# Last norms and gate of a decoder layer moved between the experts: rows in order of the later of their two experts

## The chip, the cores and the metric

The kernel runs on one core of one Trainium2 chip. The time is device time in microseconds (us) of one execution. The engines are TensorE (PE, matrix products; PEld is its loading of the stationary operand), VectorE (DVE), ScalarE (ACT), GpSimd (POOL) and SyncE (SP). Each runs its own list of instructions in order and waits for the others by semaphores. Sixteen DMA engines move data between HBM and SBUF, on behalf of SP's queue, ACT's queue and POOL's queue.

## The reference, cut to what matters

520 tokens (512 of a prompt, 8 of decoding) of width 1024 go through one layer and a last norm:

```python
m, new_buf, new_state = mixer(rmsnorm(h, g_mix), ...)        # convolution and retention heads
h = h + m
# hier_moe: top 1 of 4 groups, then top 2 of the 8 experts in it
u = rmsnorm(h, g_ffn)
for e in range(N_EXPERTS):                                    # 32
    hid = jax.nn.silu(u @ w_gate[e]) * (u @ w_up[e])          # 1024 -> 512
    y = y + cw[:, e:e + 1] * (hid @ w_down[e])                # 512 -> 1024
h = h + y
gate = jax.nn.sigmoid(rmsnorm(h, g_ple) @ w_ple_gate)         # 1024 x 1024
h = h + (p @ w_ple_proj) * gate                               # p: 256 wide, per token
y_prompt, y_sample = rmsnorm(h, g_final)
```

cw is zero for all but two experts of a token. All is float32. The weights of the 32 experts are 201 MB.

## The kernel before, in words

The **head** (to about 265 us) computes the mixer and the router, with the rows' transposes as moving operand and weights split into a high and a low part (fp32r, three products for one). At its end h lies in `xh` (token rows) and, as half rows of 512 values, in `h_rows` in HBM. The router gives for each expert the list of up to 64 rows that chose it (`index`, a row of a tile of 64; the two halves of a row lie on two partitions, so a tile is 128 x 512).

The **expert stage** takes the experts in order 0 to 31. Per expert, PE runs `gate_up` (16 matmuls of 512 columns for each of two units of weights), `hidden_t` (2 transposes), `rows_t` (4 transposes of the next expert's rows), `down` (8 matmuls, a third unit). ACT applies silu and copies the result out (`evac_out`, L908), DVE multiplies and copies (`mult_up`, `evac_h`, `evac_rows`). POOL gathers the rows of expert e+2 out of `h_rows` (L721) and scatters the result of expert e to `y_rows` in HBM (L727), which has a place for each token and each of its two choices. SP's queue loads the weights, 2 MB a unit, three units an expert. A unit is asked for as soon as the unit before it in its place has been used (`wait_ge(used[...])`). Ten places hold units at first, six ("ring", L573) from about unit 20 on. The pieces of `p @ w_ple_proj` are computed in experts 6 to 14 (L1668).

The **tail** starts when the last scatter has landed: `combine` adds the two results of each token (y_rows loaded in token order), the rows are transposed (L1938), the gate product runs in three fp32r products of 512 columns (L1964), with w_ple_gate split into high and low by ACT and DVE (L927, L1548), then sigmoid, the added projection, the last norm, and the store, for one tile of 8 and four tiles of 128 tokens. w_ple_gate is asked for at L610 behind the last expert's weights.

Order is written out by hand on each engine; there is no planner. An overflow branch (`n_over > 0`) handles experts with more than 64 rows.

Of the kernel before, what the change touches and what calls it, by code (L numbers as in the profile page):

```python
# [15 lines left out]
F32 = mybir.dt.float32  # L16
# [76 lines left out]
TAIL_TILES = [NT - 1] + list(range(NT - 1))  # L93
TAIL = [("u", 0), ("u", 1), ("pg", 0)]
for _n in range(1, NT):
    TAIL += [("pa", _n)] + ([("u", _n + 1)] if _n + 1 < NT else []) + [("pb", _n)]
TAIL.append(("pc", NT - 1))
GATES = [_job for _job in TAIL if _job[0] != "u"]
PARTS = [(_t, _q) for _t in range(NT - 1) for _q in range(2)] + [(NT - 1, 0)]
PART_FROM = 3  # L100
PART_PAIRS = -(-len(PARTS) // 2)
SPIN_TAIL, SPIN_ROWS = 52, 8


def columns_of(kind, n):

    last = n == NT - 1
    return dict(pa=slice(0, 512), pb=slice(512, 768 if last else D), pc=slice(768, D), pg=slice(0, D))[kind]


def gates(n):

    return sum(_job[1] < n for _job in GATES)

# [21 lines left out]

HEAD, REST = Plan(JOBS), Plan(TAIL)

# [5 lines left out]
GATE_SLOTS = PAIR_SLOTS[0:2]  # L144
# [8 lines left out]
def build(nc, a, o):  # L153
# [10 lines left out]
    y_tok = y_rows.rearrange("(t k) c -> t (k c)", k=2)  # L164

    with ExitStack() as ctx:
# [12 lines left out]
        def halves(ap):  # L179
# [26 lines left out]
        small = sb("small", [P, 240])  # L206
        stats = sb("stats", [P, 48])
# [10 lines left out]
                    valx=5, x0=1, y0=1, eps=1, io64=ROWS, io32=NE, rs=2, vm=4)  # L218
# [4 lines left out]
        assert at <= 240  # L223
# [43 lines left out]
        def mix_hi(k):  # L267
# [3 lines left out]
        gate_hi = [at_r(f"gate_hi{i}", UNIT, ring_at + slot * UNIT * 4)[:, :]  # L271
                   for i, slot in enumerate(PAIR_SLOTS[3:5])]
        gate_lo = [at_r("gate_lo0", UNIT, ring_at + PAIR_SLOTS[2] * UNIT * 4)[:, :], None]
        gate_lo_1 = [at_r("gate_lo10", UNIT // 2, region_d_at)[:, :],
                     at_r("gate_lo11", UNIT // 2, region_m_at + UNIT // 2 * 4)[:, :]]
        u3_hi = [at_r(f"u3_hi{i}", D, ring_at + (PAIR_SLOTS[5] * UNIT + i * D) * 4)[:, :] for i in range(2)]
        u3_lo = [at_r(f"u3_lo{i}", D, ring_at + (PAIR_SLOTS[5] * UNIT + (2 + i) * D) * 4)[:, :] for i in range(2)]
        mixT = region_m[:, :].rearrange("p (k t) -> p k t", k=KD)
        qk = region_q[:, 0:8 * T].rearrange("p (h t) -> p h t", h=8)
        pp = region_q[:, 0:NT * D].rearrange("p (t c) -> p t c", t=NT)  # L280
# [11 lines left out]
        g_fin_b = region_q[:, NT * D:NT * D + D]  # L292
        rs = [col["rs"][:, i:i + 1] for i in range(2)]
        lt16 = meanw[:, :].bitcast(F16).rearrange("p (s c) -> p s c", s=2)
        pT = trig[:, :].rearrange("p (k t) -> p k t", k=2)
# [69 lines left out]
        y_buf = [region_v[:, 0:2048], region_m[:, 0:2048]]  # L365
        u3T = [region_u[:, i * D:(i + 1) * D] for i in range(2)]
        gate = [region_u[:, 2 * D + i * D:3 * D + i * D] for i in range(2)]

        def gate_low(half, k):

            part, at = (gate_lo[0], k * 512) if half == 0 else (gate_lo_1[k // 4], k % 4 * 512)
            return part[:, at:at + 512]

# [26 lines left out]
        late_loaded, p_loaded = sem("late_loaded"), sem("p_loaded")  # L402
# [10 lines left out]
        over_hot_done, over_placed, over_done = sem("over_hot_done"), sem("over_placed"), sem("over_done")  # L413
# [12 lines left out]
        xh_loaded = [sem(f"xh_loaded{t}") for t in range(NT - 1)]  # L426
        y_loaded = [sem(f"y_loaded{i}") for i in range(2)]
        hy_done, hy_root, hy_rstd = sem("hy_done"), sem("hy_root"), sem("hy_rstd")
        gate_hi_ready, gate_lo_ready = sem("gate_hi_ready"), sem("gate_lo_ready")
        u3_ready, u3_hi_ready = sem("u3_ready"), sem("u3_hi_ready")  # L430
        pp_done, pp_made = sem("pp_done"), sem("pp_made")
        pe_tail, act_tail, dve_tail = sem("pe_tail"), sem("act_tail"), sem("dve_tail")
        part_square, part_sum = sem("part_square"), sem("part_sum")
        f_done, f_root, y_done, y_stored = sem("f_done"), sem("f_root"), sem("y_done"), sem("y_stored")
# [5 lines left out]
        def pair_fill(i, j):  # L440

            def fills(n, slot):

                return sum(16 * (PIECES if u in PIECED else 1) for u in range(n + 1) if EARLY_HOMES[u] == slot)

            if isinstance(i, int) and i < EARLY_PAIRS:
                home = EARLY_HOMES[i * 6 + j]
                if home in range(RING):
                    return home, fills(i * 6 + j, home)
                return home, 16 * len(spare[int(home[1])]) * EARLY_HOMES[:i * 6 + j + 1].count(home)  # L450
            slot = PAIR_SLOTS[j]

            return slot, i * 16 + (fills(len(EARLY_HOMES) - 1, slot) - (EARLY_PAIRS - 1) * 16)
# [3 lines left out]
        def parts_of(i, b):  # L457

            if not isinstance(i, int) or not PART_FROM <= i < PART_FROM + PART_PAIRS:
                return []  # L460
            at = (i - PART_FROM) * 2 + b
            return [at] if at < len(PARTS) else []

        def part_psum(n):

            return ps[:, 5 - n % 2, :]

        block = ctx.enter_context(nc.Block())


        @block.sync
        def _(sp):
# [126 lines left out]
            for j in range(6):  # L599
                unit, slot = NE * 3 - 6 + j, PAIR_SLOTS[j]  # L600
                sp.wait_ge(used[j % 3], NE - 2 + (j // 3 - 1))
                if j < 4:
                    load_unit(unit, slot)
# [1475 lines left out]
```

## Time and profile before

| | |
|---|---|
| time, median of 3 runs | 817.34 us (817.06 to 819.39) |
| profiled execution, span | 815.4 us |
| PE busy, DVE, ACT, POOL | 722.4, 288.1, 180.5, 102.8 us |
| DMA, all queues | 260.36 MB |
| mean granted TensorE clock | 0.986 |

The span is from the first to the last instruction; the median of the timed runs is 1.9 us above it. The profile shows three stages: the head with PE nearly always busy, the expert stage with the DMA engines nearly always busy, and the tail from 739 us on, with little DMA.

### The profile page before, as it was taken

Reading aid. Unit: us, or ns where it says so; the run is one execution under the profiler, and the core shown is the slowest. Engines: PE = TensorE matmul, PEld = TensorE weight load, DVE = VectorE, ACT = ScalarE, POOL = GpSimd, SP = SyncE. Lnnn points to the kernel's source line nnn. Section 1 sums busy time; section 2 is a strip of 40 time slices with the busy share of each in tenths; the row PEclk is TensorE's granted clock in tenths of the full one; section 3 lists DMA queues with packets and bytes.
Section 4 is the critical chain, followed back from the end, with each engine's and each line's share of the span. In section 5 each row is a group of like instructions: output and inputs, shape, how many; then the busy total and the mean of one; then the engine's idle time right before and its main releaser. Section 6 shows DMA issues by size and latency. Waiting matters only on the chain.

```text
span 815.4 us, 11407 instructions
## 1 busy us (share of the span) xinstructions
PE 722.4 (89%) x4548; PEld 454.4 (56%) x4548; DVE 288.1 (35%) x521; ACT 180.5 (22%) x276; POOL 102.8 (13%) x162
## 2 busy tenths in 40 slices
PE   8999999999999788999999987777777777788996
PEld 8999999999999433333333322222222222227785
DVE  5557888757335432110101010010011001004874
ACT  7243222223321110011111010000000000003576
POOL 0500000000001112112121211111211211100000
PEclk9999999999998899999999999999999999999998
DMA  9642127654846899999999999999999999997501
GB/s 347 244 183 79 56 88 262 254 188 154 345 137 236 317 413 410 422 425 392 426 425 427 423 426 425 428 424 429 425 426 425 428 427 424 427 416 275 205 28 78
DMA packets 38762, 260.36 MB, mean 319 GB/s; under 512 B 8161, under 2 KB 8721, under 8 KB 25657
## 3 DMA queue, kind: packets, MB, share of 16 engines
q1 hardware_dynamic: 29552, 239.27, 72.0%
q0 software_dynamic: 7072, 18.94, 6.2%
q10 hardware_dynamic: 2096, 1.56, 0.6%
q8 instruction: 31, 0.51, 0.2%
q14 instruction: 11, 0.08, 0.0%
HBM read 252.88 MB, written 15.14 MB: 329 GB/s over the span
## 4 chain that ended last, share of the span: by engine, by line
PE 60%; DMA 33%; DVE 3%; ACT 2%; issue 1%; SPq 0%; DVEq 0%; POOLq 0%; ACTq 0%
DMA arena<-in_w_exp 30%; PE ps L1625 25%; PE ps L1827 16%; PE ps L1846 6%; PE ps L1964 5%; PE ps L1668 2%; PE ps L1645 1%; DMA region_u<-h_rows,index 1%; DMA y_rows<-region_v,both_cols 1%; DMA region_q<-in_xt 1%; DVE region_u L1431 1%; PE ps L1750 1%; PE ps L1835 1%; PE ps L1938 1%; PE ps L1739 0%
## 5 line engine op out<-in xcount | busy, mean ns | idle before, releaser
L1827 PE MATMUL ps<-arena,region_u 128*64 128x512 f32 x928 | 211.5, 602 | 41.8 <-DMA arena<-in_w_exp 40.8
L1827 PEld LDWEIGHTS ps<-arena,region_u 128*64 128x64 f32 x928 | 66.4, 138 | 184.5 <-issue 132.6
L1427 DVE SCALAR_TENSOR_TENSOR region_u<-ps,small,region_u 128x256 f32<-128x256 f32 x32 | 15.5, 483 | 368.3 <-ACT region_u L904 368.3
L1625 PE MATMUL ps<-u_hi,w_hi 128*128 128x260 f32 x448 | 129.2, 288 | 2.7 <-DVE u_lo L1234 1.8
L1625 PE MATMUL ps<-u_lo,w_hi 128*128 128x260 f32 x448 | 127.5, 285 | 0.0
L1625 PE MATMUL ps<-u_hi,w_low 128*128 128x260 f32 x448 | 127.4, 284 | 0.0
L1846 PE MATMUL ps<-arena,region_u 128*64 128x512 f32 x480 | 109.6, 598 | 6.1 <-DMA arena<-in_w_exp 3.3
L1625 PEld LDWEIGHTS ps<-u_hi,w_hi 128*128 128x128 f32 x448 | 85.3, 190 | 4.0 <-DVE u_lo L1234 2.0
L1625 PEld LDWEIGHTS ps<-u_hi,w_low 128*128 128x128 f32 x448 | 85.3, 190 | 0.0
L1625 PEld LDWEIGHTS ps<-u_lo,w_hi 128*128 128x128 f32 x448 | 85.3, 190 | 0.0
L727 POOL DMA_INDIRECT y_rows<-region_v,both_cols x32 | 33.4, 1042 | 362.3 <-ACT region_v L908 362.3
L904 ACT ACTIVATE region_u<-ps,small 128x256 f32<-128x256 f32 x32 | 15.1, 473 | 258.6 <-PE ps L1827 258.6
L1846 PEld LDWEIGHTS ps<-arena,region_u 128*64 128x64 f32 x480 | 33.4, 137 | 63.0 <-issue 54.0
L908 ACT ACTIVATE region_v<-ps 128x512 f32<-128x512 f32 x32 | 19.1, 597 | 158.9 <-PE ps L1846 158.9
L1191 DVE TENSOR_TENSOR w_low<-arena,w_hi 128x1024 fp32r<-128x1024 f32 x35 | 43.3, 1237 | 15.6 <-ACT w_hi L802 15.5
L802 ACT ACTIVATE w_hi<-arena 128x1024 fp32r<-128x1024 f32 x35 | 36.8, 1051 | 26.2 <-PE ps L1625 26.1
L1625 PE MATMUL ps<-mix_lo,w_hi 128*128 128x260 f32 x128 | 36.2, 283 | 0.0
L1835 PE MATMUL ps<-ident,region_u 128*128 128x128 f32 x64 | 13.6, 294 | 25.3 <-DVE region_u L1427 25.2
L1835 PEld LDWEIGHTS ps<-ident,region_u 128*128 128x128 f32 x64 | 7.1, 141 | 50.3 <-DVE region_u L1427 48.0
L721 POOL DMA_INDIRECT region_u<-h_rows,both_cols x30 | 31.3, 1043 | 25.5 <-POOL both_cols L742 25.5
L1964 PE MATMUL ps<-gate_hi,u_hi 128*128 128x512 f32 (+1 forms) x72 | 26.7, 371 | 0.4 <-DVE u_lo L1505 0.4
L1964 PE MATMUL ps<-gate_lo,u_hi 128*128 128x512 f32 (+1 forms) x72 | 26.5, 368 | 0.0
(302 smaller groups left out, 872.8 us busy)
## 6 DMA issues: line engine op xcount, KB each, us to landing
arena<-in_w_exp SPq DMA_DIRECT2D x84, 2048.0 KB, 26.8
arena<-in_w_in SPq DMA_DIRECT2D x35, 512.0 KB, 4.3
arena<-in_w_exp SPq DMA_DIRECT2D x16, 512.0 KB, 15.7
region_q<-in_w_exp SPq DMA_DIRECT2D x24, 256.0 KB, 10.8
xh<-in_w_exp SPq DMA_DIRECT2D x8, 512.0 KB, 7.8
arena<-in_w_ple_gate SPq DMA_DIRECT2D x2, 2048.0 KB, 22.6
region_u<-in_xt SPq DMA_DIRECT2D x2, 1040.0 KB, 6.1
arena<-in_state_ret POOLq DMA_DIRECT2D x2, 1024.0 KB, 8.3
```

The source lines that it names most:

```text
L721: pool.indirect_dma_start(out=rg if rows else xg[b], out_offset=None, in_=r_rows if rows else h_rows, in_offset=bass.IndirectOffsetOnAxis( ...
L727: pool.indirect_dma_start(out=y_half, out_offset=bass.IndirectOffsetOnAxis(ap=scol[:, b:b + 1], axis=0), in_=out_sb[b], in_offset=None, bo ...
L802: nc.scalar.activation(w_hi[n % WIN_HIGH], w_raw[:, n % WIN_SLOTS, :], ACT.Copy).then_inc(w_hi_ready, 1)
L908: nc.scalar.activation(out_sb[b], ps[:, 6 + b, :], ACT.Copy).then_inc(out_sem, 1)
L1191: V.tensor_tensor(w_low[:, n % WIN_SLOTS, :], w_raw[:, n % WIN_SLOTS, :], w_hi[n % WIN_HIGH], ALU.subtract).then_inc(w_lo_ready, 1)
L1427: V.scalar_tensor_tensor(hs[b], ps[:, 2 + b, 256:512], rs[b], sg[b], ALU.mult, ALU.mult).then_inc(out_sem, 1)
L1625: last = mm(halves(out)[:, half, :], w[:, k, :], u[:, cols], start=(k == 0 and s == 0), stop=(k == KD - 1 and s == 2))
L1668: last = mm(b, pT[:, k, r0:r0 + m], w[:, k, q * 512:(q + 1) * 512], start=(k == 0), stop=(k == 1))
L1827: last = mm(ps[side * 64:side * 64 + 64, 2 + b, :], xv[:, k // 4, k % 4, :], rows(k % 4 * 2 + side), start=(k == 0), stop=(k == KD - 1))
L1835: last = tr(ps[:, 4 + b, k * P:(k + 1) * P], hs[b][:, k * P:(k + 1) * P], ident[:, :])
L1846: last = mm(ps[side * 64:side * 64 + 64, 6 + b, :], hv, rows(q * 2 + side), start=(q == 0), stop=(q == 3))
L1964: last = mm(b[:, cols], u[:, k, :], w, start=(k == 0 and i == 0), stop=(k == KD - 1 and i == 2))
```

## The change

Each token gets a key, the larger number of its two experts. Tokens are ranked by falling key and cut into nine tiles: tile 0 holds the 64 tokens with the largest keys, tile 8 the last 8. A tile is complete when the expert of its largest key is done. Tiles 8 to 2 are handled inside the expert stage, each in a fixed place (`STAGES`, tile and first expert), tiles 1 and 0 after it. Per tile: gather its rows of h and p and both its results out of `y_rows`, combine, transpose, the gate product, tanh in place of sigmoid (with a factor of a half), the added projection, the last norm, and a scatter to the output. The gate product runs with unsplit float32 operands, 64 rows at a time on two column halves, 256 columns wide (`gate_part`), and w_ple_gate stays in SBUF from unit 26 on. The last expert's result is not scattered, but added from PSUM to tile 0. `y_rows` is cleared once in the head. The loops over experts are written out. If a tile's expert is not done in time for the given routing, a flag sends the kernel to a branch that does all tiles again.

```diff
+SIDE = 64
+NS = T // SIDE + 1
+STAGES = [(8, 8), (7, 11), (6, 14), (5, 17), (4, 22), (3, 25), (2, 29)]
+LATE = [1, 0]
+ORDER = [n for n, _ in STAGES] + LATE
...
+    for i, (_, s) in enumerate(STAGES):
+        at.setdefault((s + 1, 2), []).append(("pt", i, 0))
+        at[(s + 2, 0)] = [("t", i, 0)]
+        if s + 3 < NE:
+            at[(s + 2, 2)] = [("ss", i, 0)]
+            for part in range(2):
+                at[(s + 3 + part, 0)] = [("g", i, part)]
+                at[(s + 3 + part, 1)] = [("p", i, part)]
+        else:
+            at[(s + 2, 1)] = [("ss", i, 0), ("g", i, 0), ("p", i, 0)]
+            at[(s + 2, 2)] = [("g", i, 1), ("p", i, 1)]
...
+LATE_PE = [("t", FINE, 0), ("g", FINE, 0), ("t", FINE + 1, 0), ("sum", 0, 0), ("g", FINE, 1), ("g", FINE + 1, 0),
+           ("sum", 1, 0), ("g", FINE + 1, 1), ("sum", 2, 0)]
...
+            for unit in range(10, NE * 3):
+                load_unit(unit)
+                if unit == GATE_AT:
+
+                    sp.wait_ge(gu_done, 7)
+                    sp.wait_ge(down_done, 6)
+                    for half in range(2):
+                        sp.dma_start(w_gate[half], a["w_ple_gate"][half]).then_inc(gate_loaded[half], 16)
...
+            zeros = xh[:, NT - 1, 0:832]
+            nc.gpsimd.memset(zeros, 0.0).then_inc(zeros_done, 1)
+            pool.wait_ge(zeros_done, 2)
+            pool.dma_start(y_rows.rearrange("(p r) c -> p (r c)", p=8).rearrange("a (b c) -> (a b) c", b=16).rearrange(
+                "p (n c) -> p n c", c=832), zeros.unsqueeze(1).to_broadcast([P, 10, 832])).then_inc(y_cleared, 16)
...
+            def gather_y(i, e):
+
+                n = ORDER[i]
+                for old in (e - 2, e - 1):
+                    pool.wait_ge(out_stored[old % 2], 16 * (old // 2 + 1))
+                if i >= YB:
+                    pool.wait_ge(hy_done, i - YB + 1)
+                for k in range(2):
+                    at = (k + 3) * NS + n
+                    gather(yb[i % YB][k], y_half, tix[:, at:at + 1], 4 * T - 1, y_loaded[i % 3])
...
+                for i, (n, s) in enumerate(STAGES):
+                    if e == s:
+                        gather_y(i, e)
...
+                for i, (n, s) in enumerate(STAGES):
+                    if i and e == s + 4:
+                        store_y(i - 1)
+                    if e == s - 1:
+                        gather_rows(i)
+                        gather_p(i)
+            for i in range(FINE - 2, FINE + 2):
+                store_y(i)
...
+            def roots(i):
+
+                b = piece(("ss", i, 0))
+                cols = slice(0 if i else 1, 2)
+                if i:
+                    act.wait_ge(rstd_made, i)
+                nc.scalar.activation(ssq[:, 2:4][:, cols], b[:, cols], ACT.Sqrt, scale=1.0 / D, bias=eps).then_inc(
+                    piece_act, 1)
+                back_to_silu()
...
+                if last:
+                    link(V.scalar_tensor_tensor(h, y[1], w[1], h, ALU.mult, ALU.add))
+                    dve.wait_ge(down_done, NE)
+                    V.scalar_tensor_tensor(h, ps[:, 7, :], tw[:, 2 * NS:2 * NS + 1], h, ALU.mult, ALU.add).then_inc(hy_done, 1)
...
+            def gate_part(out, u, part):
+
+                uv = u.rearrange("p (k h r) -> p h k r", h=2, r=SIDE)
+                for c in range(KD):
+                    for side in range(2):
+                        at = slice(c * 512 + part * 256, c * 512 + part * 256 + 256)
+                        last = mm(out[side * SIDE:side * SIDE + SIDE, :], uv[:, c // 4, c % 4, :], w_gate[side][:, at],
+                                  start=(c == 0), stop=(c == KD - 1))
+                return last
...
-            spin(pair(3), SPIN_TAIL)
-            for n, (kind, turn) in enumerate(TAIL):
...
-                            for i, (u, w) in enumerate(((uh, gate_hi[half][:, at]), (ul, gate_hi[half][:, at]),
-                                                        (uh, low))):
```

Where the instructions stand, at three places. In these rows, arena is the ring of weight units, in_w_exp the experts' weights, region_d and region_v buffers in SBUF, trig the new tables' region.

SP's queue of loads, from the second filling of the xh place (unit 19) to the end, before:

```order
L504 DMA xh<-in_w_exp 128x1024 x4
L573 DMA arena<-in_w_exp 128x4096 x10
L589 UNCONDITIONAL_BRANCH
L589 ISA
L573 ISA
```

```order
L573 DMA arena<-in_w_exp 128x4096 x4
L606 DMA arena<-in_w_exp 128x1024 x8
L610 DMA arena<-in_w_ple_gate 128x4096 x2
L596 DMA xh<-h_rows 128x1024
L616 TENSOR_LOAD over_expert
```

and now:

```order
L561 DMA xh<-in_w_exp 128x1024 x4
L635 DMA arena<-in_w_exp 128x4096 x7
L649 DMA xh<-in_w_ple_gate 128x4096
L649 DMA region_q<-in_w_ple_gate 128x4096
L653 DMA region_m<-in_g_final 64x512 x2
L635 DMA arena<-in_w_exp 128x4096 x67
L639 DMA arena<-in_w_exp 128x1024 x8
L659 TENSOR_LOAD over_expert
```

The 4 MB of gate weights have moved from behind the last expert's weights to behind unit 26, ahead of 69 units; the loads of h and y in token order (L596, L639) are gone from SP.

POOL's queue at two experts of the loop, before (one gather and one scatter for each expert):

```order
L721 DMA region_u<-h_rows,both_cols 128x512
L748 COPY both_cols<-index 128x1
L727 DMA y_rows<-region_v,both_cols 2080x512
L742 COPY both_cols<-index 128x1
L721 DMA region_u<-h_rows,both_cols 128x512
L748 COPY both_cols<-index 128x1
L727 DMA y_rows<-region_v,both_cols 2080x512
```

and now, from the end of expert 21 to expert 22 and on to the last two experts of the stage:

```order
L766 DMA xh<-h_rows,trig 128x512
L766 DMA region_m<-in_p_rows,trig 128x128
L750 DMA region_u<-h_rows,index 128x512
L766 DMA region_d<-y_rows,trig 128x512 x2
L772 DMA y_rows<-region_v,index 2080x512
```

```order
L772 DMA out_y<-xh,trig 1040x512
L766 DMA region_q<-h_rows,trig 128x512
L766 DMA xh<-h_rows,trig 128x512
L772 DMA y_rows<-region_v,index 2080x512
L766 DMA region_d<-y_rows,trig 128x512 x4
L772 DMA out_y<-xh,trig 1040x512
L772 DMA out_y<-region_q,trig 1040x512 x2
L772 DMA out_y<-xh,trig 1040x512
```

Per tile POOL now issues a gather of h, one of p, two of y, and a scatter to the output, among the experts' own. The scatter after the last down is gone; the four gathers of y for tiles 1 and 0 stand behind the scatter of expert 30.

ACT at the end of the kernel, before, the third tile of 128 tokens:

```order
L982 ACTIVATE region_u,stats<-xh 128x1024
L988 ACTIVATE stats<-stats,small 128x1
L1023 ACT_TABLE_LOAD
L1023 ACTIVATE region_u<-ps,stats 128x512
L974 ACTIVATE u_hi_63<-region_u 128x1024
L1023 ACTIVATE region_u<-ps,stats 128x512
```

and now, from the first half of tile 0's gate on:

```order
L1088 ACTIVATE region_v<-ps,trig 128x256
L1094 ACT_TABLE_LOAD
L1094 ACTIVATE trig<-ps,small 128x1
L1019 ACT_TABLE_LOAD
L1019 ACTIVATE trig<-small 128x1
L1113 ACTIVATE region_m,trig<-xh 128x256
L1088 ACTIVATE region_v<-ps,trig 128x256
L1116 ACT_TABLE_LOAD
L1116 ACTIVATE trig<-small 128x1
L1118 ACTIVATE region_m,trig<-xh 128x256
L1094 ACTIVATE trig<-ps,small 128x1
```

The tables for tanh and for the root take turns; the last switch (L1116) stands between the last tanh and the last square.

## Rows read from the trace of the kernel before

**Rows 1.** The page, 40 equal slices: DMA busy tenths and GB/s.
```profile
DMA  9642127654846899999999999999999999997501
GB/s 347 244 183 79 56 88 262 254 188 154 345 137 236 317 413 410 422 425 392 426 425 427 423 426 425 428 424 429 425 426 425 428 427 424 427 416 275 205 28 78
```

**Rows 2.** Windows: stretch, length, PE, PEld, DVE, ACT, POOL busy, PEclk, DMA share, GB/s.
```profile
326.00:387.00 61.00, 58.41 (x271) 20.73 (x271) 7.74 (x19) 6.07 (x11) 12.33 (x20) 1.00 1.00 414
637.00:700.00 63.00, 47.51 (x218) 16.18 (x216) 6.64 (x16) 4.28 (x8) 10.11 (x18) 1.00 1.01 426
739.00:760.00 21.00, 19.18 (x200) 16.63 (x200) 12.03 (x10) 10.32 (x9) 1.59 (x2) 1.00 0.72 280
760.00:800.00 40.00, 39.68 (x186) 32.95 (x187) 32.73 (x39) 29.40 (x44) 0.00 (x0) 1.00 0.19 72
```

**Rows 3.** Timeline of PE, experts 22, 23, 29, 30, 31: start, duration, instructions.
```profile
586.09 3.65 PE L1827 MATMUL ps<-arena,region_u 128*64 128x512 f32 x16 [1.29 <-DMA arena<-in_w_exp]
...
602.14 3.65 PE L1827 MATMUL ps<-arena,region_u 128*64 128x512 f32 x16 [1.31 <-DMA arena<-in_w_exp]
...
695.68 3.65 PE L1827 MATMUL ps<-arena,region_u 128*64 128x512 f32 x16 [1.17 <-DMA arena<-in_w_exp]
...
711.10 3.65 PE L1827 MATMUL ps<-arena,region_u 128*64 128x512 f32 x16 [1.07 <-DMA arena<-in_w_exp]
715.89 3.65 PE L1827 MATMUL ps<-arena,region_u 128*64 128x512 f32 x16 [1.15 <-DMA arena<-in_w_exp]
720.64 0.44 PE L1835 MATMUL ps<-ident,region_u 128*128 128x128 f32 x2 [1.09 <-DVE region_u L1427]
720.92 0.60 PE L1804 MATMUL ps<-ident,region_u 128*128 128x128 f32 x4
...
726.15 7.09 PE L1827 MATMUL ps<-arena,region_u 128*64 128x512 f32 x32 [0.90 <-DMA arena<-in_w_exp]
...
735.27 3.65 PE L1846 MATMUL ps<-arena,region_u 128*64 128x512 f32 x16 [0.52 <-DVE region_u L1431]
...
756.32 3.64 PE L1633 MATMUL ps<-arena,region_u 128*8 128x256 f32 x64
```

**Rows 4.** The page, DMA issues: queue, count, KB each, us to landing.
```profile
y_rows<-region_v,both_cols POOLq DMA_INDIRECT x32, 8.1
```

**Rows 5.** Timeline of ACT, DVE and POOL in the tail.
```profile
726.82 1.00 POOL L727 DMA_INDIRECT y_rows<-region_v,both_cols  x1 [14.01 <-ACT region_v L908]
...
733.27 0.47 ACT L904 ACTIVATE region_u<-ps,small 128x256 f32<-128x256 f32 x1 [7.32 <-PE ps L1827]
733.78 0.48 DVE L1427 SCALAR_TENSOR_TENSOR region_u<-ps,small,region_u 128x256 f32<-128x256 f32 x1 [11.48 <-ACT region_u L904]
...
799.63 0.69 DVE L1521 TENSOR_TENSOR region_q<-region_q,region_u 128x512 f32<-128x512 f32 x1 [1.81 <-ACT region_u L1023]
...
803.43 1.28 ACT L997 ACT_TABLE_LOAD   x1
804.72 0.29 ACT L997 ACTIVATE stats<-stats,small 128x1 f32<-128x1 f32 x1
805.03 1.28 ACT L1023 ACT_TABLE_LOAD   x1
805.05 0.16 DVE L1529 RECIPROCAL stats<-stats 128x1 f32<-128x1 f32 x1 [1.22 <-ACT stats L997]
```

**Rows 6.** The chain that ended last, from the last down on: start, us, what.
```profile
740.48 6.36 DMA y_rows<-region_v,both_cols
...
746.93 3.06 DMA region_v<-y_rows
```

More of the change, by code:

```diff
@@ L89 @@
 SPIN_FIRST = 14
[L93 to L108, printed above, removed]
@@ new lines, with bank_of, last_in @@
+AT = job_pieces()
+PIECE_READER = dict(ov="D", kr="D", tb="D", pt="D", pp="A", t="D", ss="A", g="A", p="D")
+ROLL = [job for key in sorted(AT) for job in AT[key]]
+AT_E = [key[0] for key in sorted(AT) for _ in AT[key]]
+LAST_BANKS = [1, 4, 0, 2, 6, 1]
+def bank_of(n):
+    first = AT_E.index(AT_E[n])
+    if AT_E[n] == NE - 1:
+        return LAST_BANKS[n - first]
+    return (AT_E[n] % 2, 5 - AT_E[n] % 2)[(n - first) % 2]
+def last_in(bank, e):
+    return max((n for n in range(len(ROLL)) if AT_E[n] == e and bank_of(n) == bank), default=None)
@@ L364, in build @@
                  [(xh_flat[:, n * 1024:n * 1024 + 1024], (n * 1024, n * 1024 + 1024)) for n in range(4)]]
[L365 to L372, printed above, removed]
+        w_gate = [xh_flat[:, 0:UNIT], region_q[:, 0:UNIT]]
@@ L455, in build, with home_of, filled_of @@
-        w_pp = region_z[:, 0:2 * D]
[L457 to L466, printed above, removed]
+        def home_of(unit):
+            return EARLY_HOMES[unit] if unit < len(EARLY_HOMES) else PAIR_SLOTS[unit % 6]
+        def filled_of(unit):
+            home = home_of(unit)
+            same = [u for u in range(unit + 1) if home_of(u) == home]
+            if home in range(RING):
+                return slot_filled[home], sum(16 * (PIECES if u in PIECED else 1) for u in same)
+            return spare_loaded[int(home[1])], 16 * len(spare[int(home[1])]) * len(same)
@@ new lines, in late_gated @@
+            def late_gated(i, part):
+                dve.wait_ge(late_act, LATE_ACT.index(("tanh", i, part)) + 1)
+                at = slice(part * 256, part * 256 + 256)
+                gated(i, at, late_pp[i - FINE][:, at])
+            late_u(mid)
+            take_p(last, 1)
+            combine(end, True)
+            late_u(end)
+            dve.wait_ge(late_act, LATE_ACT.index(("root", 0, 0)) + 1)
+            link(V.reciprocal(ssq[:, 14:17], ssq[:, 11:14]))
+            V.tensor_scalar(ssq[:, 15:17], ssq[:, 15:17], 0.5, None, ALU.mult).then_inc(late_dve, 1)
@@ new lines, in p_part, with rows_of @@
+            def p_part(out, pT, part, width=256):
+                for c in range(2):
+                    for side in range(2):
+                        last = mm(out[side * SIDE:side * SIDE + SIDE, :], pT[:, c * SIDE:c * SIDE + SIDE],
+                                  w_p[:, c, side, part * width:part * width + width], start=(c == 0), stop=(c == 1))
+                return last
+            def rows_of(out, h, ks):
+                for k in ks:
+                    at = (k - ks[0]) * P
+                    last = tr(out[:, at:at + P], h[:, k * P:k * P + P], ident[:, :])
+                return last
```

1072 lines of the change are left out of this document (601 added, 471 removed).

## The prediction

> **What bounds the kernel now.** I read the 40 slices first: the reader is to see that DMA is at 9 tenths or more, at some 425 GB/s, from about 285 us to about 730 us, and nearly idle behind it [rows 1]. Then the windows: in the middle of the expert stage PE is busy 58.4 of 61 us while DMA is already full, later only 47.5 of 63 us, and in the tail DMA moves 72 GB/s while PE is busy 39.7 of 40 us [rows 2]. Then PE's timeline: from expert 22 on each expert starts when its first unit of weights lands [rows 3]. So there are two bounds, one behind the other: the bytes through the DMA engines to about 736 us, then a tail of products, vector work and table switches from the end of the last down (735.27 + 3.65 = 738.9 us, [rows 3]) to 815.4 us, 76.5 us long. The change takes work out of the second and puts bytes into the first. PE's granted clock is 1.00, that is 2.4 GHz, in all of these stretches [rows 2].
>
> **The price of a byte in the expert stage.** Seven experts, 22 to 28, take (695.68 - 586.09) / 7 = 15.66 us each [rows 3]. Expert 30, in whose time no gather is made, takes 726.15 - 711.10 = 15.05 us [rows 3]. Counted with the reference's router on these inputs, an expert is chosen by 17 to 42 tokens, 32.5 in the mean; each token is two half rows of 2 KB for the gather and two for the scatter. In experts 22 to 28 these are 106 to 150 half rows an expert, in the mean 133; in expert 30 they are 50. So a half row costs (15.66 - 15.05) / 83 = 7.3 ns, and the three units alone 15.05 - 0.37 = 14.68 us, 4.89 us a unit of 2 MB. A full tile of 128 half rows (256 KB) then costs 0.94 us. From below it is the bytes at the slices' 427 GB/s, 0.61 us. From above the two ends 602.14 - 586.09 = 16.05 us with 150 half rows against 15.05 us with 50 give 10 ns, 1.28 us. I take 0.85 us, near the mean of the seven, a little below it since empty places of a tile may cost something as well and then the full ones cost less.
>
> The row shows 7.3 ns for 2 KB, that is 280 GB/s, where weights run at 429 GB/s. The Trainium skill (DMA: Bandwidth & Descriptors, Specifications) says that pieces of 512 B or more run at line rate. By that rule a tile would cost 0.61 us, and the forecast would come out some 8 us lower; this is the first rival below. The trace speaks against it, but on two stretches only.
>
> **What the change adds to DMA before the last unit lands.** (1) w_ple_gate, two units, 9.8 us; it came behind the last unit before. (2) Full tiles, each with 128 half rows: h for tiles 7 to 2 and for 1 and 0, 8; y for tiles 7 to 2, 12; stores in the loop, 4. Tile 8 has 8 tokens and costs 0.3 us in all. 24 x 0.85 = 20.4 us (14.6 to 31). (3) p, 8 tiles of 128 pieces of 512 B: between 0.15 us by bytes and 0.94 us by pieces, I take 0.35: 2.8 us (1.2 to 7.5). (4) g_final, 0.26 MB, 0.6 us. The sum is 33.9 us, from 26.5 to 49. The last unit, which lands at about 726.15 + 2 x 4.89 = 735.9 us, lands at about 770.
>
> Clearing y_rows, 4.3 MB, is asked for by POOL at about 50 us, where the slices stand at 79, 56 and 88 GB/s [rows 1]: 10 us of DMA in the shadow of PE's head, costing nothing. If it delayed the chunks of w_in it would cost up to 5 us.
>
> **What hides the added PE work.** A half of the gate is 32 instructions of 256 columns, two side by side. The few rows' gate product shows 64 such, four side by side, in 3.64 us [rows 3], and 512 columns take 3.65 us for 16 instructions, so a half takes 3.5 to 3.64; I take 3.6. With p 0.9. An expert that carries a half keeps PE busy 7.3 + 3.6 + 0.44 + 0.60 + 0.9 + 3.65 = 16.5 us, partly in gaps where PE waits for DVE now (1.09 us, [rows 3]). The DMA needs 15.66 us plus 1/3 of a tile's set (4 x 0.85 + 0.35 = 3.75 us) = 16.9 us. Two experts in three carry a half, the third only 13.3 us. So the DMA stays the bound, with little to spare in the heavy experts, and the work costs nothing there. If PE did not fit, each of the 12 heavy experts would cost about a microsecond: a rival below. The long lists of small DVE instructions in experts 1 to 3 (some 45 of about 0.2 us) may delay PE a few us; PE is then ahead of the DMA in need of data only from about expert 9 on, so this costs nothing. On POOL a tile adds five issues of 1.0 us [rows 5] in three experts; the queue behind a gather of y waits for the scatter of the expert before, 8.1 us [rows 4], which ends inside the next expert's 15.7 us, so no scatter comes late.
>
> **The new tail.** I place it on the clock of before and add the 33.9 us at the end. Gate_up of expert 31 starts at 726.15 and ends at 733.3 [rows 3]. Then t of tile 2 0.6 (it runs beside silu 0.47 and the multiply 0.48, [rows 5]), take_t and the hidden transposes to 735.1, half a gate 3.6, p 0.9: down starts at 739.8, not 735.3, and ends at 743.5. From there PE has second half and p of tile 2, 4.5; t of tile 1 0.6; 0.9 us wait for DVE; half a gate 3.6; t of tile 0 0.6; a wait of 1.3 us for combine(tile 0), which stands behind tile 2's on DVE, and for three squares; then 3.6 + 3.6 + 0.3 + 3.6: 766.1. The y rows of tile 1 are gathered once expert 30's scatter (issue 726.82, 8.1 us) is in: issued to 737, there at about 742, tile 0's at 744, before PE wants them. Behind the last half: tanh 0.5, switch to the root's table 1.28 + 0.25, square of the last half 0.65, sum 0.4, root 0.29, reciprocal 0.16, last norm 0.7, hops 0.8: 771.1. The scatter: wake-up 0.8, issue 1.0, landing. The last scatter of before takes 6.36 us from issue [rows 6] beside gate weights, a direct load 3.06 us; I take 4.1 and 1.0 for SP's end: 777. The end of before is 815.4: the tail gives back 38.4 us (34 to 41).
>
> The skill's same page (Anatomy of one DMA) puts the fixed part of a POOL transfer at about 2.0 us. By it the end would come 2 us sooner; the trace has no unloaded scatter that could show it.
>
> **Sum.** 815.4 + 33.9 - 38.4 = 810.9 us of span; the median of the runs lies 1.9 us above the span, so 812.8, said as **813 us**. Its own range is 807 to 819.
>
> **Rivals.** (a) *Half rows at the rate of bytes.* DMA adds 26.5 us instead of 33.9: 805.5 us. For it: GB/s of the slices with gathers in them hardly differ (424 to 429). Against it: the seven periods above.
> (b) *The added pieces cost more than the tail gives back*, slower than before. Place: the queues from unit 26 to 95. Price: 1.28 us a tile for 24 tiles and 7.5 us for p, 9.8 + 31 + 7.5 + 0.9 = 49 us; 815.4 + 49 - 38.4 + 1.9 = 828 us. It decides from 1.04 us a tile up (38.4 - 9.8 - 2.8 - 0.9 = 24.9, over 24), only a tenth above the mean of the seven. At the half-way price of 1.1 us, with p at 0.6, it is 821.
> (c) *PE becomes the bound in the experts with a gate half.* Inside gate_up PE still waits 1.15 us for the second unit [rows 3], so such an expert may take 18.0 us where DMA needs 16.9: 12 x 1.1 = 13 us more, 826 us. Against it: a PE that is late finds the second unit there and does not wait; the third expert of each set is light.
> (d) *A longer tail*: the root's and silu's tables take turns four times (1.28 us each) and each hop between PE, ACT and DVE counts; with 5 us more than I counted, 818 us, no change.
> (e) *The change does not do what it says*: a tile not ready in time sends the kernel to the branch with 16 more expert passes and nine tiles, over 1100 us. The router's counts speak against it: 393 tokens have their key at 8 or later where 512 may, 72 at 29 or later where 128 may, the largest expert has 42 of 64.
>
> **Chances.** Forecast 0.46, (a) 0.22, (b) 0.14, (c) 0.07, (d) 0.10, (e) 0.01. A change within 0.3%, 2.5 us, can't be told from none: 814.9 to 819.8. Faster: 0.36 of the forecast's own, all of (a), a hundredth or two of the rest, 0.60. The same: 0.10 of the forecast, nearly all of (d), 0.19. Slower: (b), (c), (e) less their lower ends, 0.21. The range, 803 to 822, takes in (a) and (d) and the lower part of (b).
>
> **What would show it.** Right: DMA at 9 tenths to about 770 us; PE waiting for in_w_exp in the light experts; the last down's end near 777; from it to the end 34 us; PE without gaps over 1.5 us between down and the last gate half. The DMA term is wrong if experts 13 to 29 take other than about 17 us in the mean; (c) shows as PE busy with no wait for in_w_exp there while DMA falls below 9 tenths; the tail term is wrong if the stretch from the last down to the end is not 31 to 38 us. What would upset all of it is a wait of expert t, g or down for a gather of y or h.

## The result, and the profile after

The changed kernel takes 811.05 us (median of four runs, 810.3 to 811.7) against 817.2 us: 0.9921 of the time before, with an interval of 0.9905 to 0.9937. That is 6.2 us or 0.8% faster, beyond the 0.3% that can be told. The profiled execution took 811.06 us with a span of 809.1 us. In two of the experiments below one execution each ran at a mean granted clock of 0.75 and took 943 to 945 us; they are left out, and since one of them was the profiled one, the trace of the run without gathers of expert rows gives its bytes but no times.

The two rows that answer to [rows 1], the page's 40 slices:

```profile
DMA  9675127653946899999999999999999999999710
GB/s 346 251 276 198 55 90 259 245 178 136 356 150 239 302 420 408 418 425 385 391 427 422 423 426 419 424 421 426 425 426 422 425 423 423 427 425 413 279 38 28
```

DMA is now at 9 tenths until slice 37, about 748 us, at the same 425 GB/s, and has 7 tenths in slice 38, so it thins out around 760 and not at the forecast 770. Before, it left the 9 tenths behind slice 36, about 734 us. The windows that answer to [rows 2] (length, busy time of PE, PEld, DVE, ACT and POOL, PE's granted clock, DMA share, GB/s):

```profile
326.00:387.00 61.00, 57.82 (x276) 20.08 (x272) 7.46 (x22) 5.97 (x11) 14.24 (x14) 1.00 1.00 404
447.00:511.00 64.00, 59.36 (x334) 24.69 (x334) 14.26 (x32) 10.14 (x20) 10.73 (x11) 0.97 1.01 424
637.00:700.00 63.00, 55.86 (x295) 22.21 (x291) 11.69 (x27) 10.93 (x22) 13.24 (x13) 0.97 1.01 424
775.00:809.00 34.00, 17.79 (x154) 11.34 (x150) 10.54 (x22) 13.98 (x28) 2.96 (x3) 0.84 0.07 25
```

Between 637 and 700 us PE is busy 8.35 us longer than it was, in time that it waited before (a part of it, some 1.7 us, is that 14 matmuls ran at the lower clock, see the last section). The DMA share there is 1.01 before and after. The last window is the stretch in which PE, before, was still in the gate's products. PE's timeline from expert 29 on, which answers to [rows 3] (start, duration, instructions, and in brackets the wait ahead and who ended it):

```profile
722.92 7.04 PE L2010 MATMUL ps<-arena,region_u 128*64 128x512 f32 x32
...
738.49 3.60 PE L2010 MATMUL ps<-arena,region_u 128*64 128x512 f32 x16
743.07 3.65 PE L2010 MATMUL ps<-arena,region_u 128*64 128x512 f32 x16 [0.97 <-DMA arena<-in_w_exp]
...
754.90 7.09 PE L2010 MATMUL ps<-arena,region_u 128*64 128x512 f32 x32 [2.09 <-DMA arena<-in_w_exp]
761.92 0.66 PE L2065 MATMUL ps<-ident,region_q 128*128 128x128 f32 x4
...
767.19 1.06 PE L2057 MATMUL ps<-region_z,region_m 128*64 128x256 f32 x8
768.06 3.63 PE L2029 MATMUL ps<-arena,region_u 128*64 128x512 f32 x16
```

Expert 31 starts at 754.90 us, 28.75 us later than in [rows 3]; its down ends at 771.69, not at 738.9. From there to the end of the span it is 37.4 us, where it was 76.5 us.

The end of the last norm and the last store, from ACT's, PE's, DVE's and POOL's timeline:

```profile
793.65 0.47 ACT L1088 ACTIVATE region_v<-ps,trig 128x256 f32<-128x256 f32 x1
794.15 1.28 ACT L1116 ACT_TABLE_LOAD   x1
...
796.48 0.36 PE L2181 MATMUL ps<-trig,region_m 128*128 128x1 f32 x2
...
797.37 0.75 DVE L1681 SCALAR_TENSOR_TENSOR xh<-xh,trig,region_m 128x512 f32<-128x512 f32 x1
799.00 0.99 POOL L772 DMA_INDIRECT out_y<-xh,trig  x1 [4.59 <-DVE xh L1681]
```

The rows of the line where each engine's program ends (duration in ns, and the start in us):

```profile
L214 DVEq DRAIN  x1: 17/17/17, 798.7 to 798.7; - x1
L214 POOLq DRAIN  x1: 8932/8932/8932, 800.0 to 800.0; - x1
...
L214 SPq DRAIN  x1: 7/7/7, 803.5 to 803.5; - x1
L214 SPq EVENT_SEMAPHORE  x1: 17/17/17, 809.1 to 809.1; - x1
```

This is the line that I had not reckoned with. SP, which waits for the last store to land, is done at 803.5 us. GpSimd issues its last scatter, is done with that at 799.99, and then drains for 8.9 us. The span ends when that is over. Before, the same drain lay inside the tail, which SP's plain stores ended:

```profile
L166 POOLq DRAIN  x1: 11342/11342/11342, 741.9 to 741.9; - x1
...
L166 SPq DRAIN  x1: 7/7/7, 815.0 to 815.0; - x1
```

### The profile page after: what moved, and what is told of

It reads as the page before. It is cut to its first block, busy times and chain, and to the rows that moved or that the text cites. A ratio compares the mean times of both kernels' runs of the same rounds, so it can differ in the third digit from the quotient of the medians.

```text
span 809.1 us, 11840 instructions
## 1 busy us (share of the span) xinstructions
PE 728.2 (90%) x4872; PEld 448.3 (55%) x4872; DVE 291.7 (36%) x609; ACT 176.8 (22%) x292; POOL 135.2 (17%) x145
## 3 DMA queue, kind: packets, MB, share of 16 engines
q0 software_dynamic: 10672, 31.49, 10.3%
## 4 chain that ended last, share of the span: by engine, by line
PE 58%; DMA 34%; DVE 4%; ACT 2%; issue 1%; SPq 0%; POOL 0%; POOLq 0%; DVEq 0%; ACTq 0%
DMA arena<-in_w_exp 32%; PE ps L1832 24%; PE ps L2010 17%; PE ps L2029 6%; PE ps L2049 4%; PE ps L2057 1%; DMA region_u<-h_rows,index 1%; DMA region_q<-in_xt 1%; PE ps L2018 1%; PE ps L1987 1%; DVE region_u L1599 0%; ACT u_hi L903 0%; ACT region_u L997 0%; PE ps L1922 0%; PE ps L1912 0%
## 5 line engine op out<-in xcount | busy, mean ns | idle before, releaser
L2010 PE MATMUL ps<-arena,region_u 128*64 128x512 f32 x928 | 213.7, 608 | 36.3 <-DMA arena<-in_w_exp 35.3
L772 POOL DMA_INDIRECT y_rows<-region_v,index x31 | 31.6, 1018 | 324.1 <-ACT region_v L1001 306.0
L2049 PE MATMUL ps<-xh,region_q 128*64 128x256 f32 x288 | 65.1, 380 | 0.9 <-DVE region_q L1738 0.8
L2049 PE MATMUL ps<-region_q 128*64 128x256 f32 x288 | 65.1, 380 | 0.0
L2049 PEld LDWEIGHTS ps<-xh,region_q 128*64 128x64 f32 x288 | 39.1, 137 | 26.1 <-issue 7.4
L2049 PEld LDWEIGHTS ps<-region_q 128*64 128x64 f32 x288 | 39.1, 137 | 0.0
L750 POOL DMA_INDIRECT region_u<-h_rows,index x32 | 32.8, 1025 | 24.1 <-issue 24.1
## 6 DMA issues: line engine op xcount, KB each, us to landing
region_q<-in_w_exp SPq DMA_DIRECT2D x24, 256.0 KB, 10.3
y_rows<-xh POOLq DMA_DIRECT2D x1, 4160.0 KB, 21.1
```

Source lines behind the costliest of these rows:

```text
L750: pool.indirect_dma_start(out=rg if rows else xg[b], out_offset=None, in_=r_rows if rows else h_rows, in_offset=bass.IndirectOffsetOnAxis( ...
L772: pool.indirect_dma_start(out=dst, out_offset=bass.IndirectOffsetOnAxis(ap=at, axis=0), in_=src, in_offset=None, bounds_check=last, oob_is ...
L2010: last = mm(ps[side * 64:side * 64 + 64, 2 + b, :], xv[:, k // 4, k % 4, :], rows(k % 4 * 2 + side), start=(k == 0), stop=(k == KD - 1))
L2049: last = mm(out[side * SIDE:side * SIDE + SIDE, :], uv[:, c // 4, c % 4, :], w_gate[side][:, at], start=(c == 0), stop=(c == KD - 1))
```

## The experiments

"E31" below is the time from expert 0's first gate_up product to expert 31's. It leaves out the head and the tail, and it is the cleaner number for what DMA costs. It is 449.7 us before, and 449.0 in the one other profile with the old expert stage. In the changed kernel it is 479.5 us in the first profile and 480.7 in the second. The other runs whose edits lie in the tail gave 479.8, 480.0 and 480.7, so 480.1 us is the mean and about 0.6 us the noise.

A word on counting: the seven tiles between the experts make 14 gathers of expert rows, but tile 8 has 8 tokens, so 12 of them are full (128 half rows) and two are small. The expectations divide by 14 and by 7; the prices below are per full gather. The page's row for GpSimd's transfers (packets, MB, share) gives the bytes. The changed kernel, then the runs without expert rows, without p, without both, and with one more gather a tile:

```profile
q0 software_dynamic: 10672, 31.49, 10.3%
q0 software_dynamic: 9552, 28.28, 8.0%
q0 software_dynamic: 10448, 31.09, 10.1%
q0 software_dynamic: 9328, 27.87, 9.3%
q0 software_dynamic: 11232, 33.09, 10.8%
```

So these runs move 3.2, 0.4 and 3.6 MB less and 1.6 MB more, which at 425 GB/s is 7.6, 0.9, 8.5 and 3.8 us. At my prices of 0.85 us a tile and 0.35 us for p it is some 10.3, 2.2, 12.5 and 5.2 us.

### The yardstick

The changed kernel once more, without an edit.

> The changed kernel once more, as the yardstick for the three runs beside it on the same chip: ratio 0.992 to the kernel before, expert 31 starting 479 to 480 us behind expert 0.

Ratio 0.9934 (0.9911 to 0.9957), span 809.6 us. It agrees with the first result within the intervals. Ratios below are read against 0.992 to 0.993.

### What a gathered row costs

No gathers of expert rows for the seven tiles between the experts:

```diff
                 for k in range(2):
                     at = (k + 3) * NS + n
-                    gather(yb[i % YB][k], y_half, ...)
+                    if i >= FINE:
+                        gather(yb[i % YB][k], y_half, ...)
...
```

> The changed kernel without the 14 gathers of experts' rows for the seven tiles finished between the experts (their sums use whatever the buffers hold; products and norms stay; two late tiles keep their gathers). Theory (DMA-bound, 12 full tiles' worth beyond what the kernel before had is what my sum charged, but here all 14 go): 14 x 0.85 = 11.9 us faster at the prediction's price of a tile of 128 rows. Since expert 31 now starts some 4 to 5 us earlier than I forecast, I expect the price below that: 9 to 10 us. Rival 'bytes alone' (0.61 us a tile): 8.5 us. Rival 'pieces, high' (1.28 us a tile): 18 us. Rival 'PE bounds the experts': 0 to 2 us.

Ratio 0.9835 (0.9807 to 0.9863): 7 to 8 us below the yardstick, 0.6 to 0.7 us a full gather. The two intervals together are about 3 us wide either way, so this run alone excludes neither price.

No gathers of p for these tiles:

```diff
...
-                        gather_p(i)
```

> The changed kernel without the seven gathers of rows of 512 B (p) for the tiles between the experts (the gate's other factor is stale for them). Prediction's term: 8 x 0.35 = 2.8 us, so 7 x 0.35 = 2.5 us faster. By bytes alone: 7 x 0.15 = 1.1 us. If a row costs its piece whatever its length (0.85 us a gather or more): 6 us or over.

Ratio 0.9939 (0.9922 to 0.9956), not to be told from the yardstick. E31 is 478.6 us, 1.5 us less: 0.25 us a full gather, between the bytes (0.15) and my price (0.35). That is two to three times the noise, so the size of this term stays rough. A price by the piece, 6 us, is out.

Both at once:

> The changed kernel without the 14 gathers of experts' rows and the 7 of p rows for the tiles between the experts (their sums use whatever the buffers hold). By bytes alone: 14 x 0.61 + 7 x 0.15 = 9.6 us less between expert 0's and expert 31's start; at my prices 14 x 0.85 + 7 x 0.35 = 14.4 us.

Ratio 0.9803 (0.9768 to 0.9838), 10.7 us under the yardstick beside it. Expert 31 starts at 744.09 us:

```profile
274.77 1.97 PE L2011 MATMUL ps<-arena,region_u 128*64 128x512 f32 x4 [0.94 <-DVE region_u L1612]
...
744.09 3.22 PE L2011 MATMUL ps<-arena,region_u 128*64 128x512 f32 x14 [1.52 <-DMA arena<-in_w_exp]
```

E31 = 744.09 - 274.77 = 469.3 us, 10.8 less than 480.1. The bytes make 8.5 of it, my prices 12.5 (the 9.6 and 14.4 of the expectation count tile 8 as full). With 1.5 us for p, 9.3 us are left for 12 full gathers, some 0.77 us each.

One more gather for each of the seven tiles (it goes over something that the tail uses, so the sums come out wrong; transfers and work on the engines are those of the changed kernel and seven gathers more):

```diff
                     gather(yb[i % YB][k], y_half, ..., y_loaded[i % 3])
+                    if i < FINE and k:
+                        gather(late_pp[i % 2], y_half, ..., y_loaded[i % 3])
...
```

> The changed kernel with one more gather of 128 expert rows for each of the seven tiles between the experts (the second expert's rows fetched once more into a buffer nobody reads then): 7 gathers more. At my price of 0.85 us: +6.0 us; by bytes alone (0.61): +4.3; if a row costs more as in the high bound (1.28): +9.0. The run without the 14 gathers was some 7 to 8 us faster than the changed kernel (0.5 to 0.56 us a gather), so I now expect +3.5 to +4.5, between expert 0's and expert 31's start.

Ratio 0.998 (0.9962 to 0.9997), 3.7 us more than the yardstick, and E31 482.9 us, 2.8 more: for six full gathers 0.47 to 0.62 us each. Taken away or added, a gather of 128 half rows costs 0.47 to 0.77 us. The 0.61 us of the bytes lies inside; 0.85 lies above all of them, though the largest comes within its noise of it.

### What a unit of gate weights costs

```diff
-        w_gate = [xh_flat[:, 0:UNIT], region_q[:, 0:UNIT]]
+        w_gate = [xh_flat[:, 0:UNIT], xh_flat[:, 0:UNIT]]
...
-                    for half in range(2):
+                    for half in range(1):
                         sp.dma_start(w_gate[half], ...)
...
```

> The changed kernel with one of the gate's two weight units loaded, and used for both sides of every gate product (the sums are wrong, the work on the engines is the same). DMA-bound: one unit of 2 MB less, 4.9 us faster. If PE bounds the experts that hold gate products, 0.

E31 is 474.4 us, 5.7 less, and the profiled span is 803.3. The ratio, 0.9912 (0.9882 to 0.9941), shows less of it: the four runs lie between 805.2 and 808.5 us. The trace stands nearer to 4.9 than to 0, but this run's size is not settled better than 1 to 6 us.

### Is PE the bound where the gate halves stand?

Two of 16 matmuls in each in-loop gate product of the first six tiles (the gates of these tiles come from one of eight parts of the sum):

```diff
-                for c in range(KD):
+                for c in ks:
...
-                    last = gate_part(b[:, 0:256], ub[i % 2], part)
+                    last = gate_part(b[:, 0:256], ub[i % 2], part, range(1) if i < FINE - 1 else range(KD))
```

> The changed kernel with 2 of 16 matmuls in each gate product of the first six tiles between the experts (12 halves of 3.45 us become 0.43 us: 36 us of PE time go; transfers, reads and all of the tail are as they were). DMA-bound: 0 to 1 us faster. Rival 'the gate products make PE the bound where they stand' (12 experts over by 1.1 us): 13 us faster.

Ratio 0.9946 (0.993 to 0.9963): nothing gained. E31 is 480.3 us. 36 us of PE work at full clock are gone and the stage is no shorter: PE waits longer, and a part of the rest runs at the lower clock.

Each of these products computed twice:

```diff
-                    last = gate_part(b[:, 0:256], ub[i % 2], part)
+                    for _ in range(2 if i < FINE - 1 else 1):
+                        last = gate_part(b[:, 0:256], ub[i % 2], part)
```

> The changed kernel with each gate product of those six tiles computed twice (12 x 3.45 us = 41 us of PE time more between the experts). How near is PE to being the bound: an expert with a gate half takes PE some 16.5 us against 16.9 of DMA by my working; with 20 us it is over by 3 us, and unless the experts without gate halves take it back, +12 x 3 = 36 us at most; if slack of neighbours absorbs it (mean PE load then under the DMA's), 0 to 10 us. The theory of a narrow margin expects +10 to +36; a wide margin expects under +3.

Ratio 1.0023 (1.0011 to 1.0034), 7 to 8 us over the yardstick; E31 486.3 us, 6.2 more. The page's row of gate_up's products shows what is left of the slack: busy time and mean, then PE's idle time ahead of them and what ended it. First the changed kernel, then the one with short and the one with doubled products:

```profile
L2010 PE MATMUL ps<-arena,region_u 128*64 128x512 f32 x928 | 213.7, 608 | 36.3 <-DMA arena<-in_w_exp 35.3
```
```profile
L2010 PE MATMUL ps<-arena,region_u 128*64 128x512 f32 x928 | 225.4, 633 | 51.3 <-DMA arena<-in_w_exp 50.3
```
```profile
L2010 PE MATMUL ps<-arena,region_u 128*64 128x512 f32 x928 | 207.5, 598 | 8.6 <-DMA arena<-in_w_exp 7.7
```

The changed kernel has 35.3 us in which PE waits for weights. Of the 12 x 3.45 = 41 us added, 27.6 went into these waits and 6.2 into E31; the rest went into shorter matmuls (the mean fell from 608 to 598 ns, since the granted clock stayed at 1.00 in this run from 280 us on, on which more below) and other waits. With the short products these waits grew by 15.0 us and the time of the same 928 matmuls by 11.7, at the lower clock. So the margin is real: some 35 us over the stage, not the few tenths of a microsecond an expert that I feared.

### What sets the end?

GpSimd waits for all nine stores before it ends:

```diff
             for i in range(FINE - 2, FINE + 2):
                 store_y(i)
+            pool.wait_ge(y_stored, 16 * len(ORDER))
```

> The changed kernel where GpSimd waits for the landing of all nine stores before it ends. If its wind-down of 8.9 us is a fixed piece of work that starts when its last instruction is done, the end is later by the wait, about 1.8 us (0.2%). If it is a wait for something that runs from the scatter's issue on (its landing, and what follows), the end stays.

```profile
L214 POOLq DRAIN  x1: 8895/8895/8895, 802.6 to 802.6; - x1
...
L214 SPq DRAIN  x1: 7/7/7, 803.2 to 803.2; - x1
```

The drain takes 8.9 us although all nine stores have landed, and the span goes from 809.1 and 809.6 to 811.7 us; ratio 0.9975 (0.9963 to 0.9987). So it does not wait for the scatter. It is a piece at the end of GpSimd's program that keeps its length when its start is moved; what it does, no run shows.

The last store by SP, as a plain transfer (the rows land at the wrong places), with GpSimd ending one store earlier:

```diff
+            sp.wait_ge(y_done, len(ORDER))
+            sp.wait_ge(y_stored, 16 * (len(ORDER) - 1))
+            sp.dma_start(out_half[0:P, :], hb[(FINE + 1) % HB]).then_inc(last_stored, 16)
+            sp.wait_ge(last_stored, 16)
...
-            for i in range(FINE - 2, FINE + 2):
+            for i in range(FINE - 2, FINE + 1):
                 store_y(i)
```

> The changed kernel with the last tile's store issued by SyncE as a plain transfer to the first 128 half rows (rows land in the wrong place; the same bytes) instead of by GpSimd as a scatter; GpSimd ends after the eighth store. With GpSimd held until all stores had landed, its wind-down took 8.9 us all the same and the span grew by 2.6 us: a fixed piece of work behind its last instruction. If so, it now starts at the issue of the eighth store (about 794.4, and ends near 803.3), and the end is set by the landing of SyncE's store and its last steps: last norm 798.1 plus about 2 us of landing plus 2 to 3 us: a span of 803 to 804, 5 to 6 us shorter. If the landing of the scatter and not GpSimd sets the end, 0 to 1 us.

```profile
L214 POOLq DRAIN  x1: 8842/8842/8842, 793.6 to 793.6; - x1
...
L214 SPq DRAIN  x1: 7/7/7, 801.8 to 801.8; - x1
```

Ratio 0.9853 (0.9818 to 0.9888), span 802.6 us: 6.5 to 7 us less, with E31 as it was (479.8 us). The last norm ends at 797.29, the span 5.3 us later, close to the 5.9 us that I had given the end. From expert 31's start to the end it takes 48.5 us where the changed kernel takes 54.2, so the wind-down of GpSimd, with the scatter in front of it, costs this kernel 5 to 6 us. Even here the drain is what ends last, at 793.6 + 8.8 = 802.4 us, 0.6 us behind SP, so a still earlier end of GpSimd would give only some tenths more. Only the runs that leave gathers out are faster, but this store does not put the rows where they belong. A version that does, with the last tile's rows sent to their places without GpSimd, wasn't tried.

### TensorE's order in the tail

```diff
-LATE_PE = [("t", FINE, 0), ("g", FINE, 0), ("t", FINE + 1, 0), ("sum", 0, 0), ("g", FINE, 1), ...
+LATE_PE = [("t", FINE, 0), ("g", FINE, 0), ("g", FINE, 1), ("t", FINE + 1, 0), ("sum", 0, 0), ...
...
```

> The changed kernel with another order on TensorE behind the last expert: both gate halves of the one late tile ahead of the transposes of the other. If TensorE runs without a gap there, the end moves by nothing; it has a wait of about 2 us before the second late tile's transposes (for the combination at the end), which the first tile's second gate half would fill: 0.7 to 3.5 us faster. If the other tile's norm or the scatter's wind-down sets the end alone: 0.

Ratio 0.9931 (0.991 to 0.9952), span 809.7: nothing. My reading of a wait of 2 us was wrong. The changed kernel's PE stops for 0.8 us at 776.6, for the evacuation of transposes, and for 0.4 us at 781.6, for ScalarE's square. In this one the first stop stays, and two others, 0.7 us at 785.3 (the evacuation behind the moved transposes) and 0.5 us at 789.6 (a square), stand in place of the second. The last gate half ends at 794.1 us instead of 793.4.

### The unsplit weights alone

In the kernel before, the tail's gate products of the full tiles with one fp32 matmul instead of three of split weights; the splitting itself is left in:

```diff
-                            for i, (u, w) in enumerate(((uh, gate_hi[half][:, at]), (ul, gate_hi[half][:, at]),
-                                                        (uh, low))):
-                                last = mm(b[:, cols], u[:, k, :], w, ...)
+                            u32 = u3T[turn % 2][:, 0:KD * m].rearrange("p (k t) -> p k t", k=KD)
+                            last = mm(b[:, cols], u32[:, k, :], ring[:, GATE_SLOTS[half], at],
+                                      start=(k == 0), stop=(k == KD - 1))
```

> One part of the change alone, in the kernel before: the tail's gate products of the full tiles as one fp32 matmul from the unsplit weights instead of three of split ones (the splitting itself by VectorE and ScalarE is left in place). A 128-row fp32 matmul over 512 columns takes 4 records, 1.91 us by the router's rows of such kind at most, or 4 x 0.2275 = 0.91 us against 3 x 0.2275 = 0.68 us of the three: over the tail's gate products slower by 8 x 2 x 0.23 = 3.7 us for each pair of tiles in the chain, together 7 to 15 us slower. If PE is not the tail's bound there: 0. The gain of the change is then in what moved out of the tail, and none of it in the unsplit weights' arithmetic.

Ratio 1.0116 (1.0094 to 1.0138), span 824.4 us: 9.5 us slower. PE is the tail's bound there and the fp32 product is the dearer one: PE is busy 55.7 us with these products, where it was 45.1. (The trace has two records a product, 144 for 72, not the four of the expectation.) The change's own form (64 rows at a time, 256 columns wide) is another shape, and no run puts it into the old tail, but its rows say the same: all gate products take PE 65.3 us in the changed kernel, against 45.1 + 3.6 = 48.8 before. So this part of the change is a cost in PE time. It pays only because the products of seven tiles moved to where PE waits for weights.

## Why the prediction came out right

The account of the two profiles, on the spans: head -1.0 us, experts 0 to 31 +29.8, and from expert 31's start to the end 54.2 where it was 89.3 us, -35.1; together -6.3 us, 815.4 to 809.1. The prediction had +33.9 and -38.4. Set against the prediction's terms:

- **The DMA term, +33.9, was too large by 4.1 us.** It measured +29.8 (30.8 between the means of five profiles and of two). Experts 13 to 29 took (722.92 - 463.47) / 16 = 16.2 us each, not 17, which was my own sign that the term is wrong. The mis-sized step is the price of a full tile, 0.85 us from the difference of experts 22 to 28 to expert 30, where the runs gave 0.47 to 0.77. A difference of 0.6 us between two stretches was too thin for a price that is used 24 times; why expert 30 was that much shorter than its neighbours stays open. Two smaller slips: tile 0's rows of h are asked for at 754.75 us, so only 23 full tiles stand in this stretch, and p cost 0.25 us a gather (rough), not 0.35.
  Rival (a), by bytes 26.5, was too low by about as much. The windows show how it adds up: from expert 0 to expert 31 DMA ran at 420 GB/s before and at 417 after, which makes 188.9 and 200.0 MB. The 11.1 MB more are 26 us at 425 GB/s; the other 3 to 4 us are the lower rate. Behind 400 us it is 423 GB/s where it was 425, which makes 1.7 us. Some 1.2 us more are lost in one place: from 385 to 390 us the DMA engines are fully busy (1.01) and move 326 GB/s. The two loads of g_final, which I had charged with 0.6 us, land there; in the run with one unit of gate weights they land some 6 us sooner, and the dip stands at 375 to 385 us (354 and 375 GB/s). No run leaves them out, so that cause is read and not shown. The Trainium skill's rule (DMA: Bandwidth & Descriptors, Specifications), that pieces of 512 B or more run at line rate, stood against my price. The runs lie around it: 0.47 to 0.77 us a tile where the bytes make 0.61. They don't settle whether a half row costs a little more than its bytes.
- **What hides the added PE work** was right, and safer than I said. Doubling the gate products lengthened the kernel by 6 to 8 us for 41 us of work; cutting them gave nothing. Rival (c) is out: PE waits 35.3 us for weights in the changed kernel. A gate half takes 32 records in 3.45 us, not 3.6.
- **The cleared y_rows** costs nothing that the profiles show. Its transfer takes 21.1 us to landing, and experts start no later. No run leaves it out.
- **The tail up to the last norm** was right: expert 31 from its start to its down's end 16.8 us (17.35 forecast), from there to the end of the last gate half 21.6 (22.6), from there to the last norm's end 4.8 (5.0). PE's longest stop up to the last gate half is 0.8 us. Its parts of the sum were 1.8 us too large. Rival (d), counted in tables and hops, did not come.
- **The end behind the last norm was too short by 5.1 us**: 5.9 forecast, 11.0 measured. I ended it with the landing of the scatter and SP's last steps; those are over at 803.5 us. Missing was GpSimd's drain, which the trace of before has at 741.9 us with 11.3 us. I had not asked what GpSimd does once its last instruction moves to the end. The experiment in which GpSimd ends one store earlier ended 5.3 us behind the last norm. The Trainium skill (DMA: Bandwidth & Descriptors, Anatomy of one DMA) gives a GpSimd transfer a fixed part of about 2.0 us beside its bytes. The trace agrees: from the start of the last scatter's issue at 799.00 to SP's first instruction behind its wait at 801.8 it is 2.8 us, of which the bytes make 0.6 at 425 GB/s. But that is not what ends the program.
- **The head** begins expert 0 about 1 us sooner: at 275.44 us, and between 273.8 and 275.0 in ten other profiles of the new layout, against 276.48 and 275.14 us in the two of the old one. The executions of one kernel differ by as much, and no run took this apart.

The errors are -4.1 (DMA), -1.0 (head), -1.8 (tail to the norm) and +5.1 us (the drain), together -1.8 us: 810.9 became 809.1. That the number is good to 2 us is in part luck: two mis-sized terms, the DMA term and the end, cancel. Without the drain the result would have lain near 805, which was rival (a)'s figure, though not by its sum alone: the head and the tail's own parts give 2.8 us of it.

## What to carry to other kernels

Work moved from a compute-bound tail into a DMA-bound stage costs little more than the bytes that it brings (here 30 us, 26 of them bytes), as long as the idle time in that stage of the engine that does the work, plus what the bytes lengthen the stage by, is larger than the work. Here PE was idle for 70.9 us between expert 0's start and expert 31's, the stage grew by 29.8 us, the work by 49.3, and 51.4 us of idle time were left. Read that idle time as one number for the whole stage, and do not judge by the fullest expert. Price a transfer by its bytes first, and let several stretches, not two, say what it costs beyond them. When a store moves to the end of a program, look at what its engine does after its last instruction: the same bytes stored through another queue, to the wrong rows, ended this kernel 6.5 us sooner.

## What was unexpected of the hardware

- GpSimd's DRAIN at the end of its program takes 8.4 to 8.9 us in all kernels of the new layout and 11.3 and 11.4 us in the two of the old one; in the changed kernel that of every other engine takes 7 to 17 ns. It does not shorten when all stores have landed.
- The granted clock of TensorE. Before, it comes up from 0.50, which is the lower level (1.2 GHz), about 282 us, at the start of the expert stage, and stays at 1.00 through the rest of it. In the changed kernel it comes up at about 280 us and falls twice to the lower level again, near 450 and 642 us (in its second profile near 500 and 681). The windows (columns as above):

```profile
443.00:448.00 5.00, 4.08 (x20) 1.18 (x16) 0.00 (x0) 0.60 (x1) 2.06 (x2) 1.00 1.03 425
448.00:453.00 5.00, 3.78 (x12) 1.21 (x14) 0.00 (x0) 0.00 (x0) 0.00 (x0) 0.69 1.00 420
453.00:458.00 5.00, 5.00 (x41) 2.60 (x37) 0.49 (x1) 0.47 (x1) 0.00 (x0) 0.96 1.02 430
```

PE's timeline there:

```profile
443.48 3.60 PE L2010 MATMUL ps<-arena,region_u 128*64 128x512 f32 x16
449.22 5.35 PE L2010 MATMUL ps<-arena,region_u 128*64 128x512 f32 x16 [2.14 <-DMA arena<-in_w_exp]
```

The fall comes right behind a wait of 2.1 us for a unit, and the 16 matmuls behind it take 5.35 us where 3.65 is usual. Other waits of that length, as the 2.09 us ahead of expert 31, have no fall behind them. With less PE work there are more falls: eight with the short gate products, none with the doubled ones. Expert 12 takes 20.0 us and expert 13 then 13.0. It cost nothing here, since DMA stayed at 1.0 and the light expert took it back; the kernel with the short gate products has a mean clock of 0.97 over 463 to 719 us against 0.99, and takes the same time. Where a fall meets PE on the path it does cost: in the run without p the clock falls at 752 us, and expert 31's gate_up products take 8.78 us instead of 7.09.
